# A dense backbone and a gathered expert layer on one core: ScalarE takes an expert group at VectorE's place of the order, TensorE one place behind it

## The chip, the cores and the metric

The kernel runs on one core of a Trainium2 chip. The metric is the device time of one execution in microseconds. The core's engines are called TensorE (PE in the profile), VectorE (DVE), ScalarE (ACT), GpSimd (POOL) and SyncE (SP); each works through its own list of instructions in order, and they meet only at semaphores.

## The reference, cut to what matters

Two layers over 512 latent tokens and 256 context tokens of width 1024, everything in fp32. Each layer has token mixers (differential attention, an mLSTM, a short convolution, merged by gates) and then a product-key expert layer, `peer`: 8 heads choose 16 of 16384 experts for each token, and

```python
def block(args):
    xb, eb, gb = args
    a = jax.nn.gelu(jnp.einsum('tkd,td->tk', u_tab[eb], xb), approximate=False)
    return jnp.einsum('tk,tkd->td', gb * a, v_tab[eb])
```

So for each of the 128 chosen experts of a token, a row of `u` and a row of `v` (1024 numbers each) are fetched from HBM, the token is multiplied with the `u` row, and the `v` rows are summed with the weight gate times gelu.

## The kernel before, in words

**Expert groups.** The expert work is cut into 20 units (64 tokens each), a unit into 32 groups, a group into 2 gathers. One gather (L1135, issued by GpSimd) brings 128 rows of `u` and `v`, 8 KB each, into one of the 8 slots of `RING`; so the ring holds 4 groups. A group then passes three engines:

- VectorE: two dot products (`tensor_tensor_reduce`, L2095), after which `dots` is counted up at L2097.
- ScalarE: waits for `dots`, then gelu (L1507), the gate's weight (L1511, twice), and a diagonal matrix (L1514, twice); L1515 counts `diag` up.
- TensorE: waits for `diag`, then 8 calls of matmul with the diagonal and the `v` halves (L819, 16 instructions in the profile), after which `slots_free` is counted up and GpSimd may refill the two slots.

**The order.** It is written out ahead. The dense work of each layer is a list of stages (norm1, qkv, da, mlp, ml, mc, mln, merge, route), each a Python generator per engine that yields after each step. `walk` runs it on every engine and, after each step, calls `group(i)` as often as `quotas()` says; i is a place in `PSEQ`, the list of all 640 groups with four empty places (`BUBBLES`) behind each of its three sequences. The groups of a step are called a row below. At place i VectorE works on group i, ScalarE on group i - `LAG_ACT`, TensorE on group i - `LAG_PE`; what is done once at the end of a unit (the sum is scaled by VectorE, L2104 and L2107, and stored by ScalarE, L1478) comes at i - `LAG_TAIL` and i - `LAG_TAIL` - 1. Each stage ends with a barrier among TensorE, ScalarE and VectorE (`phase_end`).

**The rows.** Quotas follow from the step costs in `steps()`. The dense stages that run beside groups, with the groups of each row:

```
norm1 0 (1,2): 1 0 1 1
qkv   0 (1,2): 1 1 1 2 1 1 1 1 1 0 1 2 0 1 1 1
da    0 (1,2): 1 in each of 18
mlp   0 (1,2): 0 1 0 1 0 1 1 0 1 0 1 1 0 1 0 1 1 0 1 2 1 1 1
ml    0 (1,2): 2 1 2 2 2 1 2 2
mc    0 (1,2): 1 1 1 2 1 1 1 1 2 1 1 1 1 2 1 1
mln   0 (1,2): 1 1
merge 0 (1):   1 1 0 1 1 1 1 1 1 1 1 1 0 1 1 1 1 1 1 1 1 0 1 1 1 2 1 1 1 0
route 0 (1):   3 2 2 2 2 2 2 2
merge 0 (2):   2 2 1 2 2 2 2 1 2 2 2 2 1 2 2 2 2 1 2 2 2 2 1 2 3 2 2 3 1 2
route 0 (2):   4 4 4 4 4 4 5 4
norm1, kv, mlp, ml 1 (0): 1 2 | 2 2 3 1 2 | 0 2 1 1 1 3 2 2 | 4 3 4 3
norm1, qkv, mlp, mc 1 (1): 128 groups, 8 ahead of the first step, then 2 to 6 in nearly each row
route 1 (1):   0 0 4 4 4 4 4 25
q, da 1 (2):   2 1 1 | 1 1 1 2 1 1 1 1 2
ml_on 1:       2 2
mc, mln 1 (2): 1 1 2 1 2 1 1 2 | 1
merge 1 (2):   1 1 1 1 1 1 1 1 1 1 2 1 1 1 1 1 1 1 1 1 1 1 1 1 2 1 1 2 1 1
route 1 (2):   2 2 3 2 3 2 3 2
final:         128 groups
```

The first stages up to 787 us and those from about 3630 to 4205 us have no groups beside them.

**What the dense steps need from each other.** In route, step h: TensorE makes the queries of head h + 1 (L471, 16 matmul calls), then the scores of head h (L794); ScalarE copies the queries (L1418) and the scores (L1435) out of PSUM; VectorE finds the best 16 (L1992 to L2002) and the rest of the routing (L2041 to L2067). In merge, TensorE makes one product (12 calls, L471), ScalarE its sigmoid (L1385), VectorE multiplies and adds (L1954, L1957). In da, ScalarE's exponentials are L1230, its copy L1239. In ml, TensorE's matmuls ahead for the next step are L652 and L653. In mc, TensorE's products are L471 too.

Of the kernel before, what the change touches and what calls it, by code (L numbers as in the profile page):

```python
# [25 lines left out]
SUB, PER = P // TG, TOPK * TG // P  # L26
HG = 2 * PER // GS
GROUPS = PH * HG
LAG_ACT, LAG_PE, LAG_TAIL = 1, 2, 3
BUBBLES = 4  # L30
WSLOTS, WSLOT = 3, 2304
CHUNK_NAMES = [("q", 0), ("q", 1), ("k", 0), ("k", 1), ("v", 0), ("v", 1), ("mlqk", 0), ("mlqk", 1), ("mlqk", 2), ("mlqk", 3),
# [2139 lines left out]
```

How the kernel before makes its waits and increments, by code:

```python
        @block.tensor  # L418
# [14 lines left out]
            def barrier():  # L433
                pe.drain().then_inc(s("phase_end"), 1)
                pe.wait_ge(s("phase_end"), 3 * nxt("phase_end"))
                clear.update(ROT)
# [1 line left out]
            def fill(key, n=1):  # L438
                if state["rot"] % n:
                    state["rot"] += n - state["rot"] % n
                bs = [2 + (state["rot"] + i) % 6 for i in range(n)]
                state["rot"] += n
                state["filled"] += 1
                for b in bs:
                    if b not in clear:
                        pe.wait_ge(bank_out[b], fills[b])
                    clear.discard(b)
                UNIT[key] = (bs, state["filled"], [fills[b] for b in bs])
                for b in bs:
                    fills[b] += 1
                return bs
# [4 lines left out]
            def weights(l, name, i):  # L457
                n = state["w"]
                assert CHUNKS[n] == (l, name, i), (CHUNKS[n], l, name, i)
                pe.wait_ge(w_in[n % WSLOTS], 16 * (n // WSLOTS + 1))
                state["w"] += 1
                return W_AT + (n % WSLOTS) * WSLOT
# [7 lines left out]
                for i, (a, b) in enumerate(pairs_):  # L470
                    ins = mm(out, a, b, start=(i == 0), stop=(i == last))
                return ins
            pe.wait_ge(s("const_ready"), 1)
            pe.wait_ge(s("csilu"), 1)
            for q in range(AQ):
# [359 lines left out]
            def barrier():  # L837
                sp.wait_ge(s("phase_end"), 3 * nxt("phase_end"))
```

## Time and profile before

| | |
|---|---|
| three runs | 5943.82, 5946.48, 5949.09 us; median 5946.48 |
| the profiled execution | 5943.26 us, its span 5941.0 us |
| granted clock of TensorE, mean | 0.73 |
| busy in the span: PE, DVE, ACT, POOL | 62%, 49%, 28%, 23% |
| moved from HBM | 1706.68 MB, of it 1342.26 MB by gathers |
| 5250 to 5941 us: groups 512 to 639, little else | DMA share 0.99, 398 GB/s |

No engine is busy all the time, and the four that a group passes are each the limit somewhere. A share over the whole span says little here; each stage has to be read by itself. "DMA share" is the mean busy share of the core's 16 DMA engines.

### The profile page before, as it was taken

Reading aid. Unit: us, or ns where it says so; the run is one execution under the profiler, and the core shown is the slowest. Engines: PE = TensorE matmul, PEld = TensorE weight load, DVE = VectorE, ACT = ScalarE, POOL = GpSimd, SP = SyncE. Lnnn points to the kernel's source line nnn. Section 1 sums busy time; section 2 is a strip of 40 time slices with the busy share of each in tenths; the row PEclk is TensorE's granted clock in tenths of the full one; section 3 lists DMA queues with packets and bytes.
Section 4 is the critical chain, followed back from the end, with each engine's and each line's share of the span. In section 5 each row is a group of like instructions: output and inputs, shape, how many; then the busy total and the mean of one; then the engine's idle time right before and its main releaser. Section 6 shows DMA issues by size and latency. Waiting matters only on the chain.

```text
span 5941.0 us, 64624 instructions
## 1 busy us (share of the span) xinstructions
PE 3655.9 (62%) x22248; PEld 2530.1 (43%) x22248; DVE 2908.1 (49%) x6855; ACT 1675.6 (28%) x4743; POOL 1395.3 (23%) x1297
## 2 busy tenths in 40 slices
PE   3889457788785675436455556778435787433333
PEld 1677445566664453224133235677213565311111
DVE  0321747634447544764444444321765444864444
ACT  0200127332432342233322222200224253222222
POOL 0000013212221232223334331000233222133443
PEclk7779779858887787667576668769657798655555
DMA  6434358748896898779999995114788899689998
GB/s 258 151 130 163 116 203 315 288 178 307 321 392 232 296 408 360 268 280 385 382 402 409 407 405 233 40 55 152 263 314 339 312 376 357 224 344 407 408 412 360
DMA packets 326553, 1730.30 MB, mean 291 GB/s; under 512 B 95984, under 2 KB 108624, under 8 KB 138832
## 3 DMA queue, kind: packets, MB, share of 16 engines
q0 software_dynamic: 184320, 1342.26, 57.1%
q1 hardware_dynamic: 120272, 351.64, 16.3%
q10 hardware_dynamic: 21632, 32.27, 1.9%
q8 instruction: 176, 2.88, 0.2%
q14 instruction: 153, 1.25, 0.1%
HBM read 1706.68 MB, written 19.23 MB: 291 GB/s over the span
## 4 chain that ended last, share of the span: by engine, by line
PE 39%; DMA 27%; DVE 15%; ACT 6%; issue 4%; DVEq 4%; ACTq 3%; POOL 2%; SPq 1%; PEldq 0%; POOLq 0%; PEld 0%
PE psum L471 26%; DMA arena<-in_uv,arena 22%; PE psum L819 5%; DVE arena L2095 4%; POOL arena L1135 2%; DVE arena L2002 1%; DVE arena L1995 1%; DMA arena<-in_w_ada 1%; DVE arena L1996 1%; PE psum L431 1%; PE psum L652 1%; PE psum L653 1%; ACT L1507 1%; ACT arena L1514 1%; ACT arena L1230 1%
## 5 line engine op out<-in xcount | busy, mean ns | idle before, releaser
L1135 POOL DMA_INDIRECT arena<-in_uv,arena x1280 | 1391.0, 1087 | 4511.8 <-PE psum L819 2985.4
L2095 DVE CUSTOM_DVE_ANT_0 arena<-arena 128x1024 f32<-128x1024 f32 x1280 | 1556.7, 1228 | 1378.9 <-DMA arena<-in_uv,arena 1324.2
L471 PE MATMUL psum<-arena 128*128 128x256 f32 (+2 forms) x8480 | 2027.5, 399 | 185.7 <-DVEq L1534 62.4
L819 PE MATMUL psum<-arena 128*32 128x256 f32 x10240 | 994.9, 527 | 1548.2 <-ACTq L1515 1535.0
L471 PEld LDWEIGHTS psum<-arena 128*128 128x128 f32 (+1 forms) x8480 | 1676.0, 202 | 564.6 <-issue 101.7
L819 PEld LDWEIGHTS psum<-arena 128*32 128x32 f32 x10240 | 336.4, 137 | 2116.4 <-ACTq L1515 1738.6
L1507 ACT ACTIVATE arena<-arena 128x2 f32<-128x2 f32 x640 | 131.0, 205 | 1824.1 <-DVEq L2097 1598.0
L1514 ACT ACTIVATE arena<-arena 128x32 f32<-128x32 f32 x1280 | 341.7, 314 | 45.3 <-issue 1.1
L431 PE MATMUL psum<-arena 128*128 128x128 f32 (+1 forms) x680 | 134.3, 355 | 337.3 <-DVE arena L1593 117.5
L1511 ACT ACTIVATE arena<-arena 128x1 f32<-128x1 f32 x1280 | 307.5, 287 | 45.8 <-issue 1.7
L431 PEld LDWEIGHTS psum<-arena 128*128 128x128 f32 (+1 forms) x680 | 101.9, 184 | 381.4 <-issue 166.2
L1507 ACT ACT_TABLE_LOAD x156 | 200.1, 1283 | 118.5 <-issue 57.7
L1954 DVE TENSOR_TENSOR arena<-arena,psum 128x256 f32<-128x256 f32 x120 | 50.5, 421 | 331.8 <-ACT arena L1385 326.5
L1992 DVE MAX8 arena<-arena 128x8 f32<-128x128 f32 (+1 forms) x240 | 69.6, 332 | 206.3 <-ACT arena L1435 194.7
L1385 ACT ACTIVATE arena<-psum 128x256 f32<-128x256 f32 x120 | 46.1, 384 | 301.9 <-PE psum L471 301.5
L1385 ACT ACT_TABLE_LOAD x71 | 91.1, 1283 | 58.0 <-PE psum L471 49.0
L2095 DVE DVE_READ_ACCUMULATOR2_ANT arena<- 128x1 f32 x1280 | 105.0, 82 | 0.0
L1418 ACT ACTIVATE arena<-psum 128x256 f32<-128x256 f32 x80 | 29.8, 384 | 263.5 <-PE psum L471 261.8
L1649 DVE TENSOR_REDUCE arena<-psum 128x2 f32<-128x1536 f32 (+1 forms) x40 | 61.8, 1544 | 67.2 <-PE psum L557 65.8
L557 PE MATMUL psum<-arena 64*128 64x256 f32 (+1 forms) x288 | 67.5, 588 | 37.8 <-ACT arena L1230 32.6
L572 PE MATMUL psum<-arena 128*128 128x128 f32 x416 | 67.4, 318 | 35.4 <-ACT arena L1239 35.4
L1174 ACT ACTIVATE arena<-arena 128x1024 f32<-128x1024 f32 x22 | 23.2, 1056 | 222.8 <-DMA arena<-in_ctx 89.0
(211 smaller groups left out, 2756.1 us busy)
## 6 DMA issues: line engine op xcount, KB each, us to landing
arena<-in_w_in SPq DMA_DIRECT2D x92, 1024.0 KB, 7.4
arena<-in_w_mix SPq DMA_DIRECT2D x120, 768.0 KB, 8.3
arena<-in_w_ada SPq DMA_DIRECT2D x32, 1536.0 KB, 16.3
arena<-in_w_wq SPq DMA_DIRECT2D x40, 1152.0 KB, 5.4
arena<-in_w_wo SPq DMA_DIRECT2D x20, 1024.0 KB, 8.9
arena<-in_uv,arena POOLq DMA_INDIRECT x1280, 12.5
arena<-h_rows ACTq DMA_DIRECT2D x160, 128.0 KB, 6.8
arena<-ada_rows SPq DMA_DIRECT2D x15, 512.0 KB, 7.7
```

The lines of the kernel that those rows point to most:

```text
L431: return mm(out, in_, IDENT[0:n, 0:n], start=True, stop=True, is_transpose=True)
L471: ins = mm(out, a, b, start=(i == 0), stop=(i == last))
L557: ins = mm(psum[:, 1024 + m * 1024 + a:1024 + m * 1024 + b], qt[rows, h, i * P:(i + 1) * P], KT[rows, h, a:b], start=True, stop=True)
L572: ins = mm(psum[:, 3840:3840 + P], wt[:, kt * P:(kt + 1) * P], V[:, kt, h * P:(h + 1) * P], start=(kt == 0), stop=(kt == nk - 1))
L819: ins = mm(acc_bank(u)[32 * q:32 * q + 32, gg * 256:gg * 256 + 256], DIAG[:, c, :], RING[:, sl, D + q * 256:D + (q + 1) * 256], start=(h, ...
L1135: pool.indirect_dma_start(RING[:, sl, :], None, io["uv"], bass.IndirectOffsetOnAxis(PICKED_U[b][:, h_, tg, a:a + 1], 0)).then_inc(gathered ...
L1385: A.activation(sig[:, n % 4, :], bank(b, PW), ACT.Sigmoid).then_inc(s("sig"), 1)
L1507: A.activation(GELU[:, c0:c0 + GS], ACTS[:, c0:c0 + GS], ACT.Gelu)
L1511: A.activation(WGT[:, c:c + 1], GELU[:, c:c + 1], ACT.Copy, scale=PICKED[b][:, h_, tg, PER + a:PER + a + 1])
L1514: A.activation(DIAG[:, c, :], QUAD, ACT.Copy, scale=WGT[:, c:c + 1])
L1992: V_.max(v[:, 0:8], sc)
L2095: V_.tensor_tensor_reduce(out=RING[:, sl, 0:D], in0=RING[:, sl, 0:D], in1=XT[:, gg, :], scale=1.0, scalar=0.0, op0=ALU.mult, op1=ALU.add, ...
```

## The change

All three lags become one less. ScalarE works on group i at place i, behind VectorE's dot products of the same place; TensorE on group i - 1; the ends of units come one place earlier. No instruction is added or removed, and the quotas are the same.

```diff
-LAG_ACT, LAG_PE, LAG_TAIL = 1, 2, 3
+LAG_ACT, LAG_PE, LAG_TAIL = 0, 1, 2
```

## Rows read from the trace of the kernel before

**Rows 1.** Windows: stretch, length, busy us (instructions) of PE, PEld, DVE, ACT, POOL, PEclk, DMA share, GB/s.

```profile
1377.00:1525.00 148.00, 135.99 (x816) 105.76 (x816) 68.21 (x146) 39.24 (x119) 42.10 (x38) 0.96 0.92 345
1560.00:1780.00 220.00, 188.30 (x1119) 144.81 (x1120) 96.94 (x173) 102.13 (x212) 61.57 (x54) 0.92 0.98 390
2350.00:2640.00 290.00, 120.49 (x840) 75.61 (x838) 203.64 (x648) 75.90 (x243) 71.15 (x66) 0.66 0.76 282
2900.00:3630.00 730.00, 386.41 (x2740) 216.75 (x2736) 350.14 (x605) 189.98 (x706) 271.01 (x250) 0.68 1.00 401
```

**Rows 2.** Waits: whole span; then 787:1950, 1950:2900, 4205:5250; then 1560:1780, 1950:2350, 4770:5030.

```profile
POOL arena L1135 <- PE psum L819: 2985.4, 540, 146.7
...
DVE arena L2095 <- DMA arena<-in_uv,arena: 148.9, 70, 5.7
...
DVE arena L2095 <- DMA arena<-in_uv,arena: 265.1, 146, 7.5
...
DVE arena L2095 <- DMA arena<-in_uv,arena: 213.9, 119, 7.3
...
DVE arena L2095 <- DMA arena<-in_uv,arena: 62.2, 29, 4.8
...
DVE arena L2095 <- DMA arena<-in_uv,arena: 153.5, 82, 7.5
...
DVE arena L2095 <- DMA arena<-in_uv,arena: 94.8, 49, 6.9
```

**Rows 3.** Timeline of a route step behind a row of four: start us, us, engine, operation.

```profile
2455.60 0.20 ACT L1507 ACTIVATE arena<-arena 128x2 f32<-128x2 f32 x1 [1.12 <-DVEq L2097]
...
2458.90 7.72 PE L471 MATMUL psum<-arena 128*128 128x256 f32 x32
...
2467.52 0.49 DVE L1992 MAX8 arena<-arena 128x8 f32<-128x128 f32 x2 [5.47 <-ACT arena L1435]
```

**Rows 4.** Timeline of a route step behind a row of two.

```profile
1854.94 9.30 PE L471 MATMUL psum<-arena 128*128 128x256 f32 x32
...
1870.45 0.49 DVE L1992 MAX8 arena<-arena 128x8 f32<-128x128 f32 x2
```

**Rows 5.** L1992 in 2350:2640: idle time before it, us and times; the first of the seven.

```profile
  ACT arena L1435: 58.7, 7
...
2363.49 0.49 DVE L1992 MAX8 arena<-arena 128x8 f32<-128x128 f32 x2 [16.98 <-ACT arena L1435]
```

**Rows 6.** Timeline of ml, a row of two.

```profile
1298.03 1.07 PE L819 MATMUL psum<-arena 128*32 128x256 f32 x16 [2.13 <-ACTq L1515]
...
1300.10 0.53 ACT L1514 ACTIVATE arena<-arena 128x32 f32<-128x32 f32 x2
```

**Rows 7.** Timeline of mc, a row of two behind step 8.

```profile
1458.80 7.20 PE L471 MATMUL psum<-arena 128*128 128x256 f32 x32
...
1460.16 0.21 ACT L1507 ACTIVATE arena<-arena 128x2 f32<-128x2 f32 x1 [4.38 <-DVEq L2097]
```

**Rows 8.** Timeline of da: the end of ScalarE's exponentials beside VectorE's dot products.

```profile
1001.73 0.89 ACT L1230 ACTIVATE arena<-psum,arena 128x768 f32<-128x768 f32 x1
1001.85 0.08 DVE L2095 DVE_READ_ACCUMULATOR2_ANT arena<- 128x1 f32 x1
```

**Rows 9.** Timeline of merge: ScalarE's table load and sigmoid, TensorE's group, product, next group.

```profile
1697.13 1.28 ACT L1385 ACT_TABLE_LOAD   x1
1698.42 0.38 ACT L1385 ACTIVATE arena<-psum 128x256 f32<-128x256 f32 x1
...
1700.97 1.07 PE L819 MATMUL psum<-arena 128*32 128x256 f32 x16
...
1707.37 1.07 PE L819 MATMUL psum<-arena 128*32 128x256 f32 x16
```

**Rows 10.** Timeline at the barrier behind mc.

```profile
1518.58 0.08 DVE L2095 DVE_READ_ACCUMULATOR2_ANT arena<- 128x1 f32 x1
...
1518.81 0.33 SPq L1015 DMA_DIRECT2D arena<-in_ml_norm_g  x1
```

## The prediction

> **What bounds the kernel now.** I read the page first. Its busy shares (in the table of the profile before) say that no engine is full. So I read the windows next, cut at the stages, and then the waits. The windows show three kinds of stretch [rows 1]. From 2900 to 3630 us the DMA share is 1.00 at 401 GB/s, and the last 690 us look the same: the gathers set the time, and a place in the order can give or take nothing as long as the ring is kept full. From 1377 to 1525 us PE is busy 136 of 148 us: TensorE sets the time, with its own dense products (mc; norm1, qkv and mlp before it look alike). Merge, 1560 to 1780 us, is near both limits at once (PE 188 of 220 us, DMA share 0.98). From 2350 to 2640 us (route) DVE is the busiest with 204 of 290 us, PE has 120, DMA share 0.76: VectorE sets the time, and the rest is VectorE waiting.
>
> The waits say who stands for whom [rows 2]. GpSimd waits 2985.4 us for TensorE to free slots. That looks like a ring that is freed too late, and an earlier place for TensorE would be the cure. But what it costs is seen at VectorE alone, which waits for gathers for 148.9, 265.1 and 213.9 us in the three stretches with groups beside dense work (787:1950, 1950:2900, 4205:5250), 628 us together.
>
> **What the change does.** It moves two waits. ScalarE's wait for `dots` of group i comes at place i, not i + 1, and TensorE's wait for `diag` of group i comes at place i + 1, not i + 2. Behind ScalarE's wait stand its dense copies and sigmoids, for which VectorE waits; behind TensorE's wait stand its dense products, for which both wait. The number to look at is that of groups in a row. With one group in a row TensorE meets there a group of the row before, done long ago. With two or more, the last place of the row asks for the group before the last of the *same* row, and VectorE takes that one only after its dense step. Until now it was the group before that one, which in a row of two belonged to the row before.
>
> **Route, rows of two.** Before, TensorE's queries ran during VectorE's own step: they start at 1854.94, VectorE's next step starts at 1870.45 without a wait [rows 4]. Afterwards TensorE must have that first group behind it before it starts the queries. How long that chain is, the rows of four show, where it was there already: from ScalarE's gelu of the releasing group at 2455.60 by way of TensorE's group, queries of 7.72 us from 2458.90, and the scores, to VectorE's start at 2467.52 is 11.9 us, 12.0 from the end of the dot products [rows 3]. Seven such waits in this stretch sum to 58.7 us; the first is the start of the stage, 16.98, and the one of rows 3 with its 5.47 has the end of a unit in it. The other five are 7.25 each, and with the two groups that cover them, 2.55 us each, the chain is 12.3 us [rows 5]. With queries of 9.30 us, as in rows 4, it would be 1.6 longer. After the change one group covers it in every row: a wait of 12.3 - 2.55 = 9.7 us. Rows of two whose next step has queries: five in route 0 (1), four in route 1 (2), 9 x 9.7 = 87 us. Rows of three and four lose one group of cover: 3 + 10 rows, 13 x 2.5 = 33 us. Four rows before the last head (no queries, scores alone): about 2 each, 8 us. Route: **128 us**.
>
> **Ml, rows of two.** TensorE takes the second group at 1298.03 (after 2.13 us of waiting) and then its matmuls for the step ahead, and works without a pause to the end of the step. The group that it must wait for now has its diagonals at 1300.10 to 1300.63 [rows 6]: 1300.7 - 1298.0 = 2.7 us later. Five rows of ml 0 and one of ml_on: **16 us**.
>
> **The other rows of two where TensorE sets the time.** In mc the product behind the two groups starts at 1458.80; the group that must now be done before it has its gelu at 1460.16, its diagonals 1.4 us on, its matmuls take 1 us (1.07 in [rows 6]), 0.4 passes to the product: 1463.1, 4.3 us later [rows 7]. Six such rows in the two mc: 26. Two in qkv, one of them behind the rope products (I take 8, no row of the same form) and one with VectorE idle (3): 11. One each in mlp, q, da inside: 3 x 3 = 9. Four in merge at 4, halved for the DMA limit: 8. Together **54 us**.
>
> **Rows of one.** In da ScalarE is busy without a gap; its exponentials end at 1002.62 and the dot products at 1001.93 [rows 8], so what it now waits for is there: nothing. In merge the loop closes tighter: sigmoid 0.4, VectorE's two operations 0.9 with their gaps, dot products 2.6, gelu to diagonals 1.5, the table load back to sigmoid 1.28, 6.8 with the handovers, against TensorE's 6.40 from group to group [rows 9]. 0.4 us in some 45 rows, partly under the DMA limit: **15 us**. It hangs on the price of a table switch. Here the load takes 1.28 us and the sigmoid starts 0.01 behind it (1697.13, 1698.42), 0.1 behind the diagonals.
>
> The Trainium skill ("ScalarE: Activation LUTs", What ACT_TABLE_LOAD costs) adds a drain of 1380 ns and counts 2.66 us for every switch. By that the loop in merge would be 8.2 us and the change would cost some 60 us more; the rows above show no such drain, so the sum goes without it.
>
> **Barriers.** At a stage's end VectorE's dot products were last: the barrier is passed 0.15 us after 1518.66 [rows 10]. Now ScalarE's share of the last group comes behind, 1.5 us. 22 stage ends with groups outside the stretches at the DMA limit: **33 us**.
>
> **What it gives.** Slots come free one place earlier. Of the 628 us of waits for gathers, those in the three merges, at or near the DMA limit, can't be saved: 62.2 + 153.5 + 94.8 = 310.5 [rows 2]. 317 are left, and they mostly lie where TensorE sets the time and VectorE has slack. Bounds: 0 and 317; I take 40, **-40 us**, near the lower one, because in mc PE is busy for 92% with those waits standing. The ends of units one place earlier: nothing that anyone waits for, and at most 9 us.
>
> **Sum.** 128 + 16 + 54 + 15 + 33 - 40 = 206 us. Against the profiled execution: 5943.3 + 206 = 6149; that execution is 3.2 under the median, so **6152 us**, 3.5% slower. The 20 us around it that the -40 and the halved terms leave, and a chain in route of 11.9 to 13.9 us over 22 rows (-9 to +35), give the likeliest case its own range of 6075 to 6225.
>
> **Rivals.** *The ring was the limit (faster).* One mechanism: TensorE's earlier place keeps three groups in flight instead of two, and VectorE's waits for gathers go, also in front of the dense steps. For it: 2985 us of GpSimd's waiting [rows 2]. Against: much of it falls in route, where the DMA share is 0.76 and VectorE is the busiest all the same [rows 1]. The Trainium skill ("Perfetto Trace Analysis", Optimization Strategy) reads a gap that repeats as a sign that there isn't enough room for the next tile, which speaks for this rival. It decides once more than 246 us of those 317 are saved, or if half of them are and the waits above turn out hidden: 5946 - 158 = 5788 us.
> *The waits are hidden (no change).* TensorE's clock or the weights' loading stands in front of the queries anyway, and only barriers and gains are left: 33 - 40, 5939 us. Against: the chain of [rows 3] has no DMA in it.
> *The coupling goes further (slower still).* In merge and mc gathers land late, and VectorE's waits before the groups now reach TensorE and ScalarE: the 62.2 + 94.8 us of the two merges near both limits [rows 2] on top, 6152 + 157 = 6309 us. For it: there is no slack there [rows 9]; against: gathers are issued a place (6.4 us) earlier.
> *Half the price.* Stalls of TensorE in one row are made up in the next, since a PSUM bank runs ahead: only route and half of the others (59) stay, and 60 are given back: 5946 + 128 + 59 - 60 = 6073 us.
>
> **How the numbers follow.** Likeliest case 0.60, half the price 0.19, further coupling 0.09, hidden 0.04, ring 0.08. A range of 6035 to 6245 leaves out the ring, the hidden case, and most of the further coupling. Under 0.2% (12 us) this kernel's runs tell nothing: faster 0.09, same 0.03, slower 0.88.
>
> **What would show it.** Right: VectorE idle before L1992 about 9 to 10 us behind nearly every row in all routes with groups, also where it was 0.1, and the releaser ScalarE's score copy; route 0 (1) and route 1 (2) longer by 40 to 50 us each, route 0 (2) by about 17; the stretches with a DMA share of 1.0 unchanged in length; mc and ml longer by 10 to 20 us; TensorE waiting for `diag` more. Wrong: VectorE's waits for gathers falling by over 100 us outside the two full stretches with the stages shorter, or route's queries starting early all the same. The prediction fails too if TensorE at a lower clock stretches the queries (9.30 us in [rows 4] against 7.72 in [rows 3]), which makes every 9.7 an 11.

## Result and the profile after

The changed kernel takes 6212.09 us (median of four runs, 6201.64 to 6213.35) against 5947.56 us: 1.0442 times as long, 95% interval 1.0424 to 1.0460, or 265 us more. The forecast was 6152 us with a range of 6035 to 6245, and slower with 0.88. The profiled execution after has a span of 6199.4 us against 5941.0, 258 us more.

The page after, with the span, the busy times, and the groups of the lines that take part in the change (busy, mean ns | idle before, and what ended it):

```profile
span 6199.4 us, 64622 instructions
PE 3697.0 (60%) x22248; PEld 2551.8 (41%) x22248; DVE 2893.7 (47%) x6855; ACT 1680.7 (27%) x4743; POOL 1376.1 (22%) x1297
...
L1135 POOL DMA_INDIRECT arena<-in_uv,arena x1280 | 1371.8, 1072 | 4789.3 <-PE psum L819 3277.6
...
L2095 DVE CUSTOM_DVE_ANT_0 arena<-arena 128x1024 f32<-128x1024 f32 x1280 | 1543.7, 1227 | 925.8 <-DMA arena<-in_uv,arena 828.5
...
L1954 DVE TENSOR_TENSOR arena<-arena,psum 128x256 f32<-128x256 f32 x120 | 50.6, 421 | 616.7 <-ACT arena L1385 616.7
...
L1507 ACT ACT_TABLE_LOAD x156 | 200.1, 1283 | 429.2 <-DVEq L2097 380.3
...
L1992 DVE MAX8 arena<-arena 128x8 f32<-128x128 f32 (+1 forms) x240 | 69.6, 332 | 333.4 <-ACT arena L1435 323.3
```

Nothing got more to do: VectorE's and ScalarE's busy times are within 0.5% of those of before. TensorE's rose by 41 us, from 3655.9 to 3697.0, with the same instructions, and its mean granted clock fell from 0.73 to 0.72; no run shows how much of the 265 us comes by that way. The rest is waiting. VectorE's waits for gathers (L2095) fell to 828.5 us; its waits for ScalarE's copies and sigmoids rose, at L1992 to 323.3 us and at L1954 to 616.7 us. On the page before, these three stood at 1324.2, 194.7 and 326.5 us. GpSimd waits for slots longer than before, 3277.6 us against the 2985.4 of [rows 2], though every slot is asked back one place earlier. A reader who had looked only at the waits for gathers would have called the change a gain of 496 us.

The windows after answer to [rows 1]: mc, merge of the first pair and (new here) of the second, route of the second pair, and the stretch at the DMA limit.

```profile
1450.00:1610.00 160.00, 138.87 (x813) 106.66 (x811) 64.35 (x142) 39.24 (x119) 39.22 (x38) 0.93 0.83 312
1645.00:1865.00 220.00, 188.90 (x1102) 142.96 (x1100) 94.10 (x172) 100.48 (x208) 59.84 (x52) 0.92 0.97 382
2145.00:2500.00 355.00, 239.32 (x1424) 163.56 (x1424) 146.12 (x262) 129.22 (x316) 104.75 (x96) 0.81 0.97 363
2545.00:2830.00 285.00, 97.26 (x760) 61.16 (x760) 198.06 (x617) 73.59 (x237) 66.07 (x64) 0.67 0.70 265
3090.00:3820.00 730.00, 395.64 (x2720) 218.02 (x2712) 345.18 (x600) 188.31 (x697) 261.62 (x246) 0.67 0.99 397
```

In mc, PE was busy 92% of its window and is now 87%. In the stretch at the DMA limit all columns stand within 4% of what they were. The third line is a trap: the DMA share of 0.97 looks like a stage that gathers set, but the rate is 363 GB/s. The same stage of the kernel before, from 2000 to 2340 us, reads

```profile
2000.00:2340.00 340.00, 234.25 (x1471) 162.60 (x1469) 155.36 (x267) 131.15 (x325) 113.31 (x102) 0.83 0.98 394
```

with the same share and 394 GB/s. The share hardly fell, the rate did by 8%: here it was the rate that told whether the DMA still set the pace.

From the first dot product of a stage to the first of the next, read from both timelines, the difference adds up like this (us, each number rounded by itself). Route 1 (2) has with it the 8 groups that stand ahead of the first step of the final stages.

```
                                  before   after   more
norm1 0                               24      25      1
qkv 0                                127     142     16
da 0                                 138     143      6
mlp 0                                160     174     14
ml 0                                 144     176     32
mc 0                                 156     172     15
mln and merge 0 (1), to route        276     280      4
route 0 (1)                          176     228     52
merge 0 (2)                          393     428     35
route 0 (2)                          273     284     11
all from there to route 1 (1)       1557    1556     -1
route 1 (1)                          299     305      6
q and da 1 (2)                       148     153      5
ml_on                                 16      27     11
mc 1 (2), mln, merge 1 (2)           385     387      2
route 1 (2)                          232     284     52
final stages                         650     647     -3
```

**Route.** A step behind a row of two in the timeline after; this answers to [rows 4], with all that now stands between VectorE's dot products and its next head:

```profile
1968.30 0.08 DVE L2095 DVE_READ_ACCUMULATOR2_ANT arena<- 128x1 f32 x1
1968.48 1.28 ACT L1507 ACT_TABLE_LOAD   x1 [17.35 <-DVEq L2097]
...
1970.61 0.53 ACT L1514 ACTIVATE arena<-arena 128x32 f32<-128x32 f32 x2
...
1971.22 1.94 PE L819 MATMUL psum<-arena 128*32 128x256 f32 x16 [21.51 <-ACTq L1515]
...
1973.08 8.62 PE L471 MATMUL psum<-arena 128*128 128x256 f32 x32
...
1981.54 1.05 PE L794 MATMUL psum<-arena 128*128 128x128 f32 x8
...
1982.60 0.49 DVE L1992 MAX8 arena<-arena 128x8 f32<-128x128 f32 x2 [11.69 <-ACT arena L1435]
```

Before, the queries of [rows 4] ran while VectorE still worked on its head, and TensorE had waited 4.18 us in front of them:

```profile
1853.08 1.93 PE L819 MATMUL psum<-arena 128*32 128x256 f32 x16 [4.18 <-ACTq L1515]
```

Now TensorE stands still for 21.51 us, until the row's first group has its diagonals, and only then makes 8.62 us of queries. From 1968.38 to VectorE's next start at 1982.6 the chain is 14.2 us long; the forecast had 12.3. VectorE's idle time before L1992 in route 0 (1) and route 0 (2) after:

```profile
  ACT arena L1435: 81.3, 7
...
  ACT arena L1435: 72.4, 8
```

### The profile page after: what moved, and what is told of

It reads as the page before. It is cut to its first block, busy times and chain, and to the rows that moved or that the text cites. A ratio compares the mean times of both kernels' runs of the same rounds, so it can differ in the third digit from the quotient of the medians.

```text
span 6199.4 us, 64622 instructions
## 1 busy us (share of the span) xinstructions
PE 3697.0 (60%) x22248; PEld 2551.8 (41%) x22248; DVE 2893.7 (47%) x6855; ACT 1680.7 (27%) x4743; POOL 1376.1 (22%) x1297
## 4 chain that ended last, share of the span: by engine, by line
PE 39%; DMA 19%; DVE 17%; ACT 9%; DVEq 6%; issue 4%; ACTq 3%; POOL 2%; SPq 1%; PEldq 0%; PEld 0%; POOLq 0%
PE psum L471 27%; DMA arena<-in_uv,arena 15%; DVE arena L2095 5%; PE psum L819 5%; DVEq L2097 3%; POOL arena L1135 2%; ACT arena L1514 1%; DVE arena L2002 1%; DVE arena L1995 1%; DMA arena<-in_w_ada 1%; ACT arena L1511 1%; ACT L1507 1%; DVE arena L1996 1%; PE psum L431 1%; PE psum L652 1%
## 5 line engine op out<-in xcount | busy, mean ns | idle before, releaser
L1135 POOL DMA_INDIRECT arena<-in_uv,arena x1280 | 1371.8, 1072 | 4789.3 <-PE psum L819 3277.6
L819 PE MATMUL psum<-arena 128*32 128x256 f32 x10240 | 1009.0, 532 | 1835.4 <-ACTq L1515 1823.1
L2095 DVE CUSTOM_DVE_ANT_0 arena<-arena 128x1024 f32<-128x1024 f32 x1280 | 1543.7, 1227 | 925.8 <-DMA arena<-in_uv,arena 828.5
L1954 DVE TENSOR_TENSOR arena<-arena,psum 128x256 f32<-128x256 f32 x120 | 50.6, 421 | 616.7 <-ACT arena L1385 616.7
L1507 ACT ACT_TABLE_LOAD x156 | 200.1, 1283 | 429.2 <-DVEq L2097 380.3
L1992 DVE MAX8 arena<-arena 128x8 f32<-128x128 f32 (+1 forms) x240 | 69.6, 332 | 333.4 <-ACT arena L1435 323.3
L2095 DVE DVE_READ_ACCUMULATOR2_ANT arena<- 128x1 f32 x1280 | 105.2, 82 | 0.0
L1385 ACT ACT_TABLE_LOAD x71 | 91.1, 1283 | 50.3 <-PE psum L471 41.6
L1812 DVE SCALAR_TENSOR_TENSOR arena<-psum,arena 128x128 f32<-128x128 f32 x80 | 22.5, 344 | 141.6 <-PE psum L653 141.6
## 6 DMA issues: line engine op xcount, KB each, us to landing
arena<-in_uv,arena POOLq DMA_INDIRECT x1280, 11.7
```

What stands on the lines that cost most here:

```text
L819: ins = mm(acc_bank(u)[32 * q:32 * q + 32, gg * 256:gg * 256 + 256], DIAG[:, c, :], RING[:, sl, D + q * 256:D + (q + 1) * 256], start=(h, ...
L1135: pool.indirect_dma_start(RING[:, sl, :], None, io["uv"], bass.IndirectOffsetOnAxis(PICKED_U[b][:, h_, tg, a:a + 1], 0)).then_inc(gathered ...
L1385: A.activation(sig[:, n % 4, :], bank(b, PW), ACT.Sigmoid).then_inc(s("sig"), 1)
L1507: A.activation(GELU[:, c0:c0 + GS], ACTS[:, c0:c0 + GS], ACT.Gelu)
L1992: V_.max(v[:, 0:8], sc)
L2095: V_.tensor_tensor_reduce(out=RING[:, sl, 0:D], in0=RING[:, sl, 0:D], in1=XT[:, gg, :], scale=1.0, scalar=0.0, op0=ALU.mult, op1=ALU.add, ...
```

## Experiments

"Before" in the ratios is always the first kernel on the same chip. A ratio is estimated from the runs of both kernels and stands with its 95% interval; it lies up to 0.0013, 8 us, beside the ratio of the two medians. Differences in us between two experiments are those of their medians, so a few us of them mean nothing.

### ScalarE alone moved (e1_act_only)

```diff
-LAG_ACT, LAG_PE, LAG_TAIL = 1, 2, 3
+LAG_ACT, LAG_PE, LAG_TAIL = 0, 2, 3
```

> Lags 0, 2, 3: only ScalarE's place is moved, TensorE stays two places behind. Theory (the price is TensorE's wait for a group of its own row in front of dense products): only the barriers (some 22 x 1.5 us), the merge loop and a copy that comes 1.5 us late in route are left, 50 to 90 us over the kernel before, 5998 to 6038 us, and VectorE's waits for ScalarE's score copy in route stay below 3 us behind rows of two. Rival (ScalarE, stuck behind VectorE's dot products with its copies and sigmoids, carries the price): 180 us or more, over 6130 us.

Measured: 5962.06 us, 1.0016 (1.0004 to 1.0028), 10 us by the ratio and 16 by the medians, less than the theory's own 50. VectorE's waits for the score copy behind rows of two were 2.5 to 2.8 us, as the theory had them, but for two of 4.6 and 4.7 us in route 0 (1). The rival is out: ScalarE stuck behind VectorE's dot products costs next to nothing by itself. The step from here to the changed kernel, TensorE (with the unit ends) one place earlier, costs the other 250 us. The waits show that a sum of waits is no price. VectorE's wait for the sigmoid is already most of what it is in the changed kernel, and the kernel is 0.2% slower than before:

```profile
DVE arena L2095 <- DMA arena<-in_uv,arena: 1058.7, 681, 8.2
DVE arena L1954 <- ACT arena L1385: 511.1, 118, 12.9
```

By stages, the routes with rows of two (0 (1) and 1 (2)) are 17 and 16 us longer, ml 0 is 12 us *shorter* (132 against 144), and the merges 0 (2) and 1 (2) are 6 us shorter each.

### TensorE alone moved (e2_pe_only)

```diff
+LAG_ACT, LAG_PE, LAG_TAIL = 1, 1, 2
```

> Lags 1, 1, 2: only TensorE's place is moved; it takes a group at the place at which ScalarE does. Theory: TensorE meets the same group of its own row as in the changed kernel, so route costs its 120 us again, ml and mc theirs, and the barriers' share stays away: 150 to 220 us over the kernel before, 6100 to 6170 us. Rival (ScalarE carries the price): under 80 us, below 6030 us.

Measured: 6669.66 us, 1.1209 (1.1186 to 1.1233). Far outside both. The experiment was not what I took it for: with ScalarE and TensorE at the same place, TensorE waits for what ScalarE makes at that very place, in rows of one group too. What it undoes is the place of distance between the two, which the change keeps. From its waits, against 1535.0 us of the same name before:

```profile
PE psum L819 <- ACTq L1515: 2199.4, 572, 41.1
```

So it doesn't tell TensorE's part apart, but it gives the price of no distance: 12%. What TensorE's earlier place costs is known only together with ScalarE's and with that of the unit ends.

### Old places in single stages

For this `walk` notes the stage in `now[0]`, and the two `group` functions of TensorE (shown) and ScalarE count their own progress and ask for their lag by the stage. Where the lag changes between two stages, an engine takes two groups at one place, or none, so the edges of a stage are those of neither kernel. The unit ends keep the places of the kernel before.

```diff
+        def lag_now():
+            kind, l, pairs = now[0] or ("", 0, ())
+            return (1, 2) if kind == "route" else (0, 1)
...
-                item = PSEQ[i - LAG_PE] if i >= LAG_PE else None
-                if item is None:
+                while pe_at[0] <= i - lag_now()[1]:
+                    one(PSEQ[pe_at[0]])
+                    pe_at[0] += 1
+
+            def one(item):
+                if item is None:
```

> The changed kernel, but in the four route stages ScalarE and TensorE keep their old places (one and two behind), with unit ends three places behind. Theory: the 120 us that the route stages grew by come back whole: 6080 to 6105 us against 6212, and VectorE's waits before its first maximum are as in the kernel before (0.1 us behind rows of two). Rival (the route's growth only hides what would be lost elsewhere, in the gathers): under 60 us come back.

Measured: 6091.68 us, 1.0235 (1.0212 to 1.0257), 120 us under the changed kernel. The 121 us that the four route stages grew by came back whole, and the wait before the first maximum has in sum and number what it had before (194.7 us, 21 times):

```profile
DVE arena L2012 <- ACT arena L1449: 194.7, 21, 20.0
```

The same means the other way round, new places in one stage of the kernel before:

```diff
+            return (0, 1) if (kind, l, pairs) == ("merge", 0, (2,)) else (1, 2)
```

> The kernel before, but in the merge stage of the second pair of layer 0 alone (rows of two groups, DMA share near 1) ScalarE and TensorE take the new places. Theory (a loop from the sigmoid over the dot products, the diagonals, TensorE's groups and the next product, 13.3 us, takes the place of the 11.5 us that the gathers need for a row): 25 to 45 us slower, 5972 to 5992 us. Rival (the stage is set by the DMA and its growth came from what lies before it): no difference beyond 10 us.

Measured: 5987.59 us, 1.0061 (1.0039 to 1.0082), 42 us by the medians, 23 to 49 by the interval; in the trace the stage is 40 us longer. The stage alone does it.

```diff
+            return (0, 1) if kind in ("ml", "ml_back", "ml_on") else (1, 2)
```

> The kernel before, with the new places in the mLSTM stages alone (ml and ml_on). The prediction gave these rows of two 16 us; the traces of the two kernels differ by 32 us in ml 0 and 11 in ml_on. Theory (TensorE's wait is longer than the sum had it, because VectorE's own step stands in front of the group that it asks for): 25 to 50 us slower, 5973 to 5998 us. Rival (only the 16 us are this mechanism, the rest comes in from stages before): 5955 to 5968 us.

Measured: 5981.72 us, 1.0061 (1.0045 to 1.0078), 31 us by the medians, 27 to 46 by the interval; in the trace ml 0 is 31 us longer and ml_on 10. The rival's 16 us are excluded by little (its upper edge of 5968 lies at a ratio of 1.0029).

```diff
+            return (0, 1) if (l, pairs) == (1, (1,)) and kind in ("norm1", "qkv", "mlp", "mc") or kind == "final" else (1, 2)
```

> The kernel before, with the new places only where the DMA share is 1.0: norm1, qkv, mlp and mc of the second pair of layer 1, and the final stages (256 of the 640 groups). Theory: nothing, within 8 us of the kernel before. Rival (freeing slots a place earlier helps where gathers set the time): 20 us faster or more.

Measured: 5947.35 us, 0.9997 (0.9986 to 1.0007). Where the DMA is full, 256 of the 640 groups, the change does nothing that the runs can tell (8 us faster to 4 us slower), as the forecast had it.

And the changed kernel with the old places in the three kinds of stage at once:

```diff
+            return (1, 2) if kind in ("route", "ml", "ml_on") or (kind, l, pairs) == ("merge", 0, (2,)) else (0, 1)
```

> The changed kernel with the old places in route, in ml and ml_on, and in the merge of the second pair of layer 0. Singly these were worth 120, 31 and 42 us. Theory (separate mechanisms that add): 6212 - 193 = 6019 us, 6005 to 6035. Rival (they overlap, and what one gives up another takes): 6060 us or more.

Measured: 6032.52 us, 1.0136 (1.0120 to 1.0153), 180 us under the changed kernel. The single effects sum to 193, so they add nearly whole. In the trace the first mc, behind ml with its old places, is 180 us long against 172 in the changed kernel, which takes 8 of the 13 us. 1.36%, 81 us, is what all other stages cost together.

### The queries before the row's groups (e3_after_hoist, e4_before_hoist)

If the chain through the queries is the price in route, it can be cut without touching a lag: TensorE makes the queries of head h + 2 before row h.

```diff
                 queries(0)
+                queries(1)
                 for h in range(PH):
-                    if h + 1 < PH:
-                        queries(h + 1)
                     scores(h)
+                    if h + 2 < PH:
+                        queries(h + 2)
                     yield
```

> The changed kernel, with the queries of head h + 2 made before the groups of row h in route, not behind them. Between the releasing group and VectorE's next head only the scores (1 us) are left. Theory: the chain of 12.3 us shrinks to about 5, VectorE's wait from 10 us to 2 or 3 behind 22 rows: 150 to 180 us come back, 6035 to 6065 us. Rival (the loop goes through ScalarE, whose copies stand behind its wait for the dot products): VectorE still waits 7 us or more and under 60 us come back.

Measured, in the changed kernel: 6074.73 us, 1.0206 (1.0186 to 1.0225), 137 us less than without, a little short of the theory's 150. The wait before the first maximum falls from 323.3 to 169.1 us; behind the rows that have queries after them it is now mostly 2.5 us, as the theory had it:

```profile
DVE arena L1993 <- ACT arena L1436: 169.1, 30, 20.4
```

> The kernel before with the same reordering of the queries. Theory: the waits of 5.5 to 9.2 us behind rows of three and four go, 13 of them, 80 to 95 us: 5853 to 5870 us, faster than both kernels. Rival (TensorE has no room for the queries beside VectorE's head, or the weights come too late for them): under 30 us.

Measured, in the kernel before: 5895.26 us, 0.9914 (0.9894 to 0.9935), 53 us faster, between the theory's 80 and the rival's 30. In the second pair's route VectorE's waits for the score copy shrink to 4.5 us, the start of the stage aside, but part of it returns as waits for gathers, because TensorE now stands before queries whose weights have not come, with the row's groups behind it:

```profile
DVE arena L2096 <- DMA arena<-in_uv,arena: 19.1, 7, 7.4
...
DVE arena L1993 <- ACT arena L1436: 4.5, 2, 2.5
...
PE psum L471 <- DMA arena<-in_w_wq: 19.0, 4, 15.1
```

### TensorE one place further behind (e7_pe_later)

```diff
+LAG_ACT, LAG_PE, LAG_TAIL = 1, 3, 4
+BUBBLES = 5
```

> Lags 1, 3, 4, with five empty places behind a sequence in place of four: TensorE goes one place further behind, the opposite of the change. Theory: rows of three and four in route get another group of cover (13 x 2.5 us), ml's rows of two lose their wait of 2 us, but a slot of the four groups is freed a place later and VectorE waits more for gathers in merge: between 40 us faster and 20 us slower, 5905 to 5965 us. Rival (the ring is the limit, so that each place further behind costs): over 60 us slower.

Measured: 6038.99 us, 1.0154 (1.0137 to 1.0171). A miss for the theory and right for its rival. Three places of distance leave one group of the ring in flight, and VectorE waits for gathers 1644.7 us, the longest wait twice that of before:

```profile
DVE arena L2095 <- DMA arena<-in_uv,arena: 1644.7, 915, 15.2
```

So the ring is a limit on that side: three places cost 1.5%. That more room than two places leave would bring anything, no run shows.

### What each engine can bear, put together (e9_hoist_act_part)

```diff
+            return (0, 2) if kind in ("ml", "ml_on", "mc", "merge") else (1, 2)
```

with the queries early as above.

> The kernel before with the queries made before the row's groups in route, and ScalarE at VectorE's place in ml, mc and merge alone; TensorE keeps two places everywhere. With ScalarE alone moved, ml 0 was 12 us shorter than before, the merges 5 to 6 us each, mc 2, and only route was longer. Theory: these add to the gain of the queries: 5860 to 5885 us. Rival (the differences between two traces are chance or shift elsewhere): as with the queries alone, 5890 to 5900 us.

Measured: 5873.99 us, 0.9884 (0.9865 to 0.9904). 1.2% faster than before, the fastest kernel of the study. The gain over the early queries alone (21 us by medians of runs on different chips; the two intervals overlap from 0.9894 to 0.9904) is likely but not shown.

## Why the prediction was right, and where its sum was off

**Route: right in mechanism and size.** Forecast 128 us, measured 120. The chain was longer than 12.3 us in rows of two (14.2 above, with TensorE's queries at 8.62 us and a table load in front). The waits before the first maximum rose by 323.3 - 194.7 = 128.6 us. That every row, also those with 0.1 us before, would show about 10 us, and that the score copy would be the releaser, is what the trace after has for rows of two: 9.5 to 11.7 us. Rows of four are mostly a little under the forecast, at 8.1 to 8.6. So the two routes with rows of two grew by 52 us each, a little over the forecast's 40 to 50, and route 0 (2) by 11, under its 17.

**Merge of the second pair: the step that failed.** The forecast took the merges out of the sum: "those in the three merges, at or near the DMA limit, can't be saved", and no price but the 15 us of rows of one and 8 of rows of two was set for them. A stage at the DMA limit gained nothing here, but it can lose, as soon as a loop through the engines gets longer than the transfers. With rows of two this loop runs over both groups. The timeline after has a whole turn of it:

```profile
2253.84 1.07 PE L819 MATMUL psum<-arena 128*32 128x256 f32 x16
2253.94 0.38 ACT L1385 ACTIVATE arena<-psum 128x256 f32<-128x256 f32 x1 [5.15 <-PE psum L471]
...
2255.46 1.23 DVE L2095 CUSTOM_DVE_ANT_0 arena<-arena 128x1024 f32<-128x1024 f32 x1
...
2258.73 0.53 ACT L1514 ACTIVATE arena<-arena 128x32 f32<-128x32 f32 x2
...
2259.34 1.94 PE L819 MATMUL psum<-arena 128*32 128x256 f32 x16 [4.43 <-ACTq L1515]
...
2261.20 6.20 PE L471 MATMUL psum<-arena 128*128 128x256 f32 x24
...
2267.44 0.38 ACT L1385 ACTIVATE arena<-psum 128x256 f32<-128x256 f32 x1 [4.21 <-PE psum L471]
```

Sigmoid, VectorE's product and the first group's dot products, its diagonals, TensorE's group, TensorE's next product, sigmoid: 2267.44 - 2253.94 = 13.5 us. Two groups and a weight block are 4.19 + 0.79 MB, at the 401 GB/s of the full stretch in [rows 1] an estimated 12.4 us. The 1.1 us between them, in the 24 rows of two or more, would be 26 us of the 35 in the table. VectorE waits for no gather in that turn; over the stage its idle time went from gathers (149.8 us before) to the sigmoid (165.4 us after). In e6_new_lags_in_merge02 this stage alone gave 42 us. The serial loop had been worked out in the prediction for rows of one only.

**Ml: right in mechanism, half in size.** 16 us forecast, 31 measured. The sum held TensorE's wait for the diagonals at 2.7 us over before. Two rows of the trace after:

```profile
1321.89 1.28 ACT L1507 ACT_TABLE_LOAD   x1 [4.44 <-DVEq L2097]
...
1324.62 1.93 PE L819 MATMUL psum<-arena 128*32 128x256 f32 x16 [6.49 <-ACTq L1515]
...
1346.31 1.28 ACT L1507 ACT_TABLE_LOAD   x1
...
1351.71 1.93 PE L819 MATMUL psum<-arena 128*32 128x256 f32 x16 [4.80 <-ACTq L1515]
```

The second has 4.80 us against the 2.13 of [rows 6], 2.67 more and so the forecast's 2.7. The first has 6.49, and most of the rest is the table load. In the second row ScalarE loads at once and then waits for `dots`; in the first the load itself waits for them. The diagonals that the prediction took its time from, those of 1300.10 in [rows 6], were made without a load in front. Over the whole stage (1235 to 1379 us before, 1272 to 1448 after) TensorE's wait went from 12.1 to 38.8 us:

```profile
PE psum L819 <- ACTq L1515: 12.1, 6, 2.7
...
PE psum L819 <- ACTq L1515: 38.8, 6, 9.7
```

TensorE's own work in it took longer too:

```profile
1235.00:1379.00 144.00, 116.09 (x625) 90.65 (x626) 73.93 (x179) 41.04 (x103) 33.07 (x28) 0.57 0.54 197
...
1272.00:1448.00 176.00, 127.67 (x625) 99.51 (x625) 73.22 (x179) 41.45 (x104) 30.54 (x28) 0.50 0.46 163
```

The same 625 matmuls were busy for 11.6 us more, with a mean granted clock of 0.50, the lower of its two levels, against 0.57. The prediction had no term for it. The 26.7 us of waits and these 11.6 are more than the 32 by which the stage grew, so they overlap in part, and no run separates them.

**The rows of two in TensorE's stages, the rows of one and the barriers** were 54 + 15 + 33 us, less 40. Together they had 62 us; the runs left 81 for them. Singly they are not all shown. In da nothing was forecast, and its stage grew by 6 us; qkv had 11 and grew by 16, mlp 3 and 14, the two mc 26 and 22 (15 and 6, the first dot product of mc to that of mln). In qkv it is the mechanism of the forecast: TensorE's wait for the diagonals went from 3.7 us (811 to 937 us before) to 19.0 (812 to 955 after). In mlp 0 and mc 0 it rose by 9 and 10 us, less than the stages grew by.

```profile
PE psum L819 <- ACTq L1515: 3.7, 3, 2.0
...
PE psum L819 <- ACTq L1515: 19.0, 5, 8.5
```

The barrier itself was priced well:

```profile
1602.94 0.08 DVE L2095 DVE_READ_ACCUMULATOR2_ANT arena<- 128x1 f32 x1
...
1603.90 0.53 ACT L1514 ACTIVATE arena<-arena 128x32 f32<-128x32 f32 x2
1604.55 0.33 SPq L1015 DMA_DIRECT2D arena<-in_ml_norm_g  x1
```

1.53 us from the end of the dot products to the passed barrier, against the 0.15 of [rows 10]. But 22 of them, 33 us, are more than the whole kernel lost with ScalarE alone moved (1.0016, 10 us, in which the two routes with rows of two had 33 of their own). That kernel gains in ml, because TensorE finds the diagonals of the row before ready and its wait of 2.13 us goes, and in the merges; how much of the barriers' price is covered by this and how much never was on the path, the runs don't tell apart.

**What it gives.** I took 40 us of the 317. Outside the full stretches the waits for gathers fell from 628 us to 63.4 + 86.8 + 79.8 = 230, so 398 us of them went, and the kernel became slower. The prediction named a fall by over 100 us *with* shorter stages as the sign that it was wrong; the first half came, the second did not. In e1_act_only, too, they fell, over the whole span from 1324.2 to 1058.7 us, and the kernel did not get faster: their sum was no measure of what could be gained.

**The table switch.** The Trainium skill ("ScalarE: Activation LUTs", What ACT_TABLE_LOAD costs) counts 2.66 us for a switch. The trace after doesn't agree: a load takes 1283 ns in all 156 cases in front of gelu, and in the step of route above it starts at 1968.48 and gelu follows at 1969.78, 0.02 us behind its end.

**The rivals.** The ring as the limit: out for the change's direction (e10_new_lags_dma_full, and 398 us less waiting without a gain), true in the other (e7_pe_later). Hidden waits and half the price: out by the measured time. The coupling that goes further was the one that came partly true, in a merge, by the loop and not by late gathers.

**The number.** 265 us were measured against the 206 of the sum. By the runs, the merge was missing with 42, ml with 15, the other stages with 19, and route had 8 too many; that makes 68 and not 59, as single effects overlap a little. Three of the four errors have one sign, so the number is not right by their cancelling; 6212 lies in the upper part of the stated range. The range of the likeliest case, 6075 to 6225, doesn't follow from its terms: 20 and 9 us down and 20 and 35 up from 6152 give 6123 to 6207, and the measured time lies just above that.

## What to carry to other kernels

The distance in places between engines that share an order written by hand is cover for what stands *behind* a wait, not for the wait. Before shortening it, write down for each stage which dense instruction stands behind the moved wait and how many groups of the same row now come before it: in route a row of two groups lost 10 us, while mln and the 30 steps of merge 0 (1), nearly all with one group or none, lost 4 us together. Not every stage of such rows was that cheap (mlp 0 lost 14). Engines can be moved apart: here ScalarE's wait could move for 0.2%, ScalarE's and TensorE's together cost 4.4%, and moving the long dense work (the queries) in front of the wait was worth more than any lag. A stage at its DMA limit gained nothing from an earlier place, but one near it lost 42 us.

## What the runs showed of the hardware

**A table load can stand behind the wait it should hide under.** All 156 loads in front of gelu take 1283 ns. In the timeline before, at 1701.48, the load ran at once, and the ACTIVATE at 1704.11 did the waiting, 1.34 us. Behind others ScalarE is idle until `dots` and loads only then, as here in merge after:

```profile
2243.27 1.28 ACT L1507 ACT_TABLE_LOAD   x1 [3.12 <-DVEq L2097]
...
2254.34 1.28 ACT L1507 ACT_TABLE_LOAD   x1
...
2257.91 0.21 ACT L1507 ACTIVATE arena<-arena 128x2 f32<-128x2 f32 x1 [2.28 <-DVEq L2097]
```

Counted over the traces, loads that waited for `dots` were 12 before and 46 after, 45 of these and all 12 in front of each head's first group (every fourth), where the code has a second wait, for `picked`, before that for `dots`. In all other places the code has one wait and but one load waited. 34 loads more at 1.28 us are up to 44 us by themselves. But with ScalarE alone moved 45 loads waited for `dots` as well, and that kernel lost 10 us in all, so most of them cost little there. That the loads wait because of two waits in a row is read from the pattern, no run took the second wait away.

**The DMA share didn't fall when the rate did.** In the merge of the second pair the share was 0.98 at 394 GB/s before and 0.97 at 363 GB/s after. The packets in the traces of those two windows (2000 to 2340 and 2145 to 2500 us) show one reason: an 8 KB packet of a gather took 324 ns in the mean before and 342 ns after, though the median fell from 313 to 309. The packets over 600 ns went from 0.5% to 3.1%, and they count as busy all the while. So the GB/s beside the share has to be read too; what held them up is not shown.
